# Row chunks of a sparse expert stage: none beside the last twelve one-hot groups of the u pass, six more in the v pass

## What is computed

```python
e = (take(i1, ci // 16) * 128 + take(i2, ci % 16))   # 128 picked experts of a token
g = softmax(sc)                                       # their gates
a = gelu(einsum('nd,nhkd->nhk', xb, u[e]))            # u, v: (16384, 1024)
y = einsum('nhk,nhkd->nd', g * a, v[e])
x = x + y
```

## Time and profile before

| | us |
|---|---|
| median of three runs | 2267.19 (2264.80 to 2267.72) |
| the profiled execution | 2267.32 |
| its span, first to last instruction | 2265.7 |
| PE busy | 2104.7 (93%) |
| DVE busy | 1340.9 (59%) |
| POOL busy | 555.2 (25%) |
| ACT busy | 360.4 (16%) |

### The profile page before, as it was taken

How to read it: one execution, slowest core, us unless ns; L and a number is a source line. 1 busy time by engine, 2 the same in 40 slices (tenths; PEclk the granted TensorE clock), 3 DMA queues, 4 the chain that set the end, 5 groups by cost and what they waited for, 6 DMA issues and landing times. The chain is left out here.

```text
span 2265.7 us, 24748 instructions
## 1 busy us (share of the span) xinstructions
PE 2104.7 (93%) x8855; PEld 1573.0 (69%) x8855; DVE 1340.9 (59%) x2881; ACT 360.4 (16%) x745; POOL 555.2 (25%) x516
## 2 busy tenths in 40 slices
PE   6968989976999999899999999999799999999987
PEld 4745577753788976677777777777467777777776
DVE  2005377763436238679999999888635365455233
ACT  1001146641001111211111222222000000000011
POOL 1001100012000000233245555454433353443000
PEclk9988999987559999999999999999899999999998
DMA  3142221113113332387889999999999999999521
GB/s 129 38 68 76 74 93 56 38 43 107 47 56 126 124 114 100 129 288 287 292 305 361 410 401 394 399 405 404 402 378 330 380 374 383 397 342 358 186 80 61
DMA packets 166864, 511.69 MB, mean 226 GB/s; under 512 B 18285, under 2 KB 52725, under 8 KB 163158
## 3 DMA queue, kind: packets, MB, share of 16 engines
q1 hardware_dynamic: 93782, 273.61, 33.7%
q0 software_dynamic: 60288, 213.96, 24.7%
q10 hardware_dynamic: 12672, 22.55, 2.6%
HBM read 460.32 MB, written 49.72 MB: 225 GB/s over the span
## 5 line engine op out<-in xcount | busy, mean ns | idle before, releaser
L1935 PE MATMUL ex_ps<-proj,ex_ring 128*128 128x320 f32 x2048 | 557.0, 435 | 22.5 <-DMA ex_ring<-in_v 22.5
L1880 PE MATMUL ex_ps<-h,ex_ring 128*128 128x320 f32 x2048 | 566.9, 434 | 5.9 <-DMA ex_ring<-in_uT 5.9
L1935 PEld LDWEIGHTS ex_ps<-proj,ex_ring 128*128 128x128 f32 x2048 | 391.7, 191 | 187.5 <-DMA ex_ring<-in_v 23.7
L1880 PEld LDWEIGHTS ex_ps<-h,ex_ring 128*128 128x128 f32 x2048 | 384.7, 191 | 157.0 <-DMA ex_ring<-in_uT 6.1
L2111 DVE TENSOR_TENSOR proj<-proj 128x320 f32<-128x320 f32 x124 | 53.0, 490 | 253.2 <-DMA proj<-scratch_a 233.2
L2045 DVE SCALAR_TENSOR_TENSOR gx_sum<-proj,gx_sum 128x1024 f32<-128x1024 f32 x120 | 154.2, 1285 | 9.2 <-DVE gx_sum L2045 0.9
L2027 DVE CUSTOM_DVE_ANT_0 proj<-proj,gx_tokens 128x1024 f32<-128x1024 f32 x120 | 143.9, 1223 | 3.5 <-DMA proj<-in_u,at_last 3.1
L1782 POOL DMA_INDIRECT scores<-in_u,at_last x26 | 31.2, 1202 | 453.3 <-POOLq L1501 404.6
L1788 POOL DMA_INDIRECT proj<-in_v,at_last x76 | 105.1, 1383 | 84.2 <-DVE gx_sum L2045 68.3
L1782 POOL DMA_INDIRECT proj<-in_u,at_last x76 | 88.2, 1160 | 143.9 <-DVE proj L2027 131.4
L379 PE MATMUL gate_ps<-h,work 128*128 128x260 f32 x512 | 120.3, 389 | 3.1 <-DMA work<-in_w_t 3.1
(11 more groups left out here) (386 smaller groups left out, 2768.1 us busy)
## 6 DMA issues: line engine op xcount, KB each, us to landing
ex_ring<-in_uT SPq DMA_DIRECT2D x128, 512.0 KB, 6.7
ex_ring<-in_v SPq DMA_DIRECT2D x128, 512.0 KB, 6.8
scratch_a<-ex_gelu ACTq DMA_DIRECT2D x64, 320.0 KB, 7.2
scratch_w<-proj SPq DMA_DIRECT2D x10, 2048.0 KB, 12.4
proj<-scratch_a SPq DMA_DIRECT2D x15, 1280.0 KB, 9.7
proj<-scratch_w SPq DMA_DIRECT2D x15, 1280.0 KB, 10.7
work<-in_w_t SPq DMA_DIRECT2D x37, 512.0 KB, 3.6
mg_ring<-in_w_q SPq DMA_DIRECT2D x32, 512.0 KB, 3.4
```

The costliest lines, as they stand in the source:

```text
L1880: last = nc.tensor.matmul(y[:, bank(n), 0:TD], u[:, n % UR, k, :], xn[:, k, 0:TD], start=(k == 0), stop=(k == DC - 1))
L1935: last = nc.tensor.matmul(y[:, m, 0:TD], ring[:, (E1 + e) % UR, m * P:(m + 1) * P], hidden_of(part_of[e])[:, e - parts[part_of[e]][0], :], ...
```

## The change

The last twelve one-hot groups (68 to 79) have no `dot` and no `add` behind them on DVE. U_CHUNKS falls from 54 to 48, and with it ACT's list of small gelus in the u pass; the other 52 chunks are spread over the 32 quads of v by the same formula, 48 + 52 * (q + 1) // 32. Nothing is added or left out: the six chunks, with their 24 gathers, are made later.

```diff
     PRE_CHUNKS = 14
-    U_CHUNKS = PRE_CHUNKS + NG // 2
+    QUIET = 12
+    U_CHUNKS = PRE_CHUNKS + (NG - QUIET) // 2
@@
             for g in range(NG):
                 rows(g)
+                if g >= NG - QUIET:
+                    continue
                 if g % 2 == 0:
                     dot(chunk + 1)
                 else:
```

## The result

The changed kernel is slower: 2275.79 us (median of five, 2274.27 to 2280.15) beside 2267.01 of the kernel before, a ratio of 1.0047 with a 95% interval of 1.0036 to 1.0058, or 8 to 13 us. Forecast was 2260.8, and 2252 to 2271 as the range.

The account below looks back on a forecast made before the run. PE was taken as the bound, with the loss in its waits where u passes into v. The gate block's 7.7 us earlier hidden(1), of which 6.5 survive to tile 9, turned 2267.32 into 2260.8 us, range 2252 to 2271.

Parts of the forecast that it names:

- PE as the bound: Experts stage: PE is busy nearly throughout u and v; what is lost lies in 22.5 us of waits in v.
- DVE's work hidden: End of u: DVE drops six chunks, 30 us, which PE hid, so this gains nothing.
- the gate block: u's last block of gates reaches DRAM in 7.5 us instead of 15.2, so hidden(1) goes out 7.7 us earlier.
- Tile 4: Early v: starts 16.7 us after hidden(1) plus 0.4 for gather overlap; PE waits 6.6 us instead of 12.8.
- Weights(3) and tile 9: Early v: weights(3) leaves after quad 2's products, tile 9 starts 24.1 us later; 6.5 us of the 7.7 survive.
- the seam: Passage from the u pass to the v pass, where PE waits ahead of tiles 0, 4 and 9; gain 6.5 us.
- Into v: Middle of v: the moved chunks cost nothing; a four-chunk part runs 3.1 us over, worked off in the next two.
- The second one, four-chunk parts: Rival, chance 0.13: in parts 6, 10 and 14 gathers slow the next weights load; 2291 us, or 2271 at a third.
- Sharing by packets: DMA queues take turns packet by packet, so 1 KB weights rows lose to 4 KB gathers; used for tile 9's lateness.

Follow-up runs that it names:

- e1: The changed kernel with v's chunks dealt out as one beside part 0, three beside each full part, six beside the last: 2261.5 us, ratio 0.9979.
- e4: The changed kernel with v's chunks dealt out as none beside part 0, three beside each full part, seven beside the last: 2253.6 us, ratio 0.9944.
- e6: The changed kernel with four one-hot groups cleared instead of twelve, no chunks beside part 0, one each beside parts 1 and 2, seven beside the last: 2243.3 us.
- e9: The changed kernel with five chunks in parts 6, 10 and 14, two in the part ahead of each, three beside the last: 2299.1 us, ratio 1.0158.
- e5: The changed kernel with gates in DRAM in reading order: weights loads in 10 KB runs, each block stored in three transfers of 1 KB runs: 2275.3 us.
- e3: The changed kernel with four one-hot groups cleared instead of twelve, so two chunks leave u instead of six: 2262.3 us, ratio 0.9985.

## Why the prediction was wrong

*PE as the bound, DVE's work hidden, the gate block.* Right. The block landed after 7.3 us, where 7.5 was assumed, and hidden(1) went out 7.9 us earlier relative to the block's issue.

*Tile 4.* Mis-sized. The term was 17.1 us from hidden(1), and it was 21.4. I took most of part 0's four gathers as already counted in the 16.7 us of the kernel before and added 0.4 us, where the bound allowed 2. In the kernel before they had left 5.8 us and more ahead of hidden(1); now they left from 2.8 us ahead of it to 2.0 behind, onto weights(1) and (2) with their 1 KB rows. There they cost 4.7 (20.3 against 15.6 us in e1 and e4), and the bound itself was too narrow, since it went by bytes.

*Weights(3) and tile 9.* Right in the order: weights(3) left at 1614.16, as quad 2's products ended, and tile 9 began 23.0 us after it (24.1 assumed). But weights(1) landed late beside the same gathers, so part 1's products began later, and weights(3) left 30.0 us after hidden(1) instead of the 25.6 of the sum. So the seam gained 3.5 us instead of 6.5. e6 shows what tile 9 waited for: the gathers of parts 1 and 2.

*Into v.* This is the step that failed. I counted the overrun of a four-chunk part, 3.1 us of its 34.45, found the 12.9 us of lead and the 6.8 of a median tile, and took nothing; it cost 15.4 us. The argument against, that no middle part had waited at 97% DMA, says nothing about how near a wait was. A row would have: before, part 6's last gather left 7.7 us ahead of the weights, and one chunk more takes POOL 6.4 us (four chunks' 16 gathers went out in 23.0 us in the changed kernel, three chunks' 12 in 16.6 before). That leaves some 1 us, and it was 0.5, where the part's last gather landed 15.7 us after its issue.

*The rival.* The second one, four-chunk parts, is what happened, in the three parts that it named, by the mechanism that it named, with chance 0.13. Its price was 10.2 us for each part in full, waiting and lower clock together, and 3.4 at a third. The changed kernel paid 5.1 for each, half of it (3.9, 3.0 and 3.3 of waiting), and e9, with five chunks, 12.5 for each. Its ends, 2271 and 2291, were worked out with 6.5 us of gain. With the measured 3.5 the mild end is 2274, and the range I gave ended at 2271.

*Sharing by packets.* The rule that stands in the prediction from the Trainium skill, "DMA: Bandwidth & Descriptors", Queues, rings and completion order, agrees with e5: the bytes and the chunks were the same, the weights' rows ten times longer, and the late waits fell from 10.3 to 0.35 us. I used it for tile 9 alone and not where it spoke against the change, on every weights load of v.

## What to carry to other kernels

An average load of 390 of 405 GB/s says little: work that comes in bursts has to be laid against the transfers that follow it, part by part, and the distance between the last of the one and the first of the other is the margin to read before work is moved. A rounded spread, k * (q + 1) // n, makes some parts larger than others; a number that divides evenly, or the rest put where the queue is idle, kept the gain of the move (e1, e3) that the changed kernel lost. Transfers with short rows suffered most beside a queue of long ones, so they are what to keep the bursts away from, or to lengthen where the other end can bear it, which the stores of e5 could not.

## What the runs showed of the hardware

Two DMA queues that both had work passed nearly equal numbers of packets, and from weights(3) on a load of 1.31 MB in 1 KB rows took 17 to 26 us where gathers of 4 KB rows went out right up to its issue or on behind it, and 8.1 us at best; with rows of 10 KB it took 13 to 14 beside as many gathers (e5, parts 6, 10 and 14). That the sharing goes by packets was expected. That a transfer of short runs can hold the engine that issues it was not: weights(2), 1280 runs of 1 KB, held SP for 8.7 us in the changed kernel, with gathers beside it, and for 2.6 in e4, without them; one store of 1 KB runs in e5 held it for up to 9.5. What SP had to issue next left that much later, and in e5 this went with tiles of u that were late by 13 us.
